# Gate and up of five feed-forward stages: three pairs of steps as seven block products, with weight sums on VectorE

## What is computed

```
def swiglu_2(x, w_gate, w_up, w_down):
    return (jax.nn.silu(x @ w_gate) * (x @ w_up)) @ w_down

def macaron_ffn(xs, g, shift, scale, gate, w_gate, w_up, w_down):
    return xs + 0.5 * gate * swiglu_2(modulate(xs, g, shift, scale), w_gate, w_up, w_down)
```

## Time and profile before

| what | value |
|---|---|
| median of 3 runs | 3579.99 us (3577.64 to 3580.52) |
| span of the profiled execution | 3574.0 us |
| TensorE busy (matmul) | 3487.5 us, 98% of the span, 18564 matmuls |
| VectorE busy | 2211.7 us, 62% |
| ScalarE busy | 1712.6 us, 48% |
| GpSimd busy | 113.8 us, 3% |
| mean granted TensorE clock | 0.997 of full |
| DMA | 654.63 MB, 183 GB/s over the span |

### The profile page before, as it was taken

One profiled execution on the slowest core, in us unless ns is written; L12 is line 12 of the kernel. 1 busy time (PEld: TensorE's weight loads), 2 busy tenths in 40 slices (PEclk: granted clock), 3 DMA queues, 4 the chain that ended last, 5 costly groups with the idle time before them and its releaser, 6 DMA issues. The chain is left out here.

```text
span 3574.0 us, 45127 instructions
## 1 busy us (share of the span) xinstructions
PE 3487.5 (98%) x18564; PEld 2960.8 (83%) x18564; DVE 2211.7 (62%) x2603; ACT 1712.6 (48%) x2073; POOL 113.8 (3%) x116
## 2 busy tenths in 40 slices
PE   9999999999999998999999999999999999999999
PEld 7889888888888887888889878888888678888887
DVE  5776656676667677576677555555556555545655
ACT  5454454544645446545454354545453454545543
POOL 0001100000000000000001100000000000000000
PEclk9999999999999999999999999999999999999999
DMA  7642156664476763676742145555554135454453
GB/s 271 239 154 79 60 202 234 216 231 176 156 271 252 258 226 123 224 282 227 280 178 93 60 177 189 182 184 183 183 175 154 60 142 189 172 189 164 156 209 130
DMA packets 90554, 654.63 MB, mean 183 GB/s; under 512 B 10096, under 2 KB 10224, under 8 KB 11632
## 3 DMA queue, kind: packets, MB, share of 16 engines
q1 hardware_dynamic: 79344, 574.15, 44.2%
q0 software_dynamic: 11008, 77.60, 6.0%
HBM read 650.66 MB, written 1.05 MB: 182 GB/s over the span
## 5 line engine op out<-in xcount | busy, mean ns | idle before, releaser
L2013 DVE TENSOR_TENSOR w_lo<-raw,w_hi 128x2048 fp32r<-128x2048 f32 x540 | 1234.2, 2290 | 614.5 <-ACT w_hi L1382 614.3
L1382 ACT ACTIVATE w_hi<-raw 128x2048 fp32r<-128x2048 f32 (+1 forms) x542 | 1032.7, 1909 | 499.2 <-PE acc L584 401.1
L582 PE MATMUL wrk<-w_hi,h_hi 128*128 128x512 f32 (+1 forms) x2400 | 939.6, 391 | 15.8 <-issue 5.4
L584 PE MATMUL wrk<-w_hi,h_lo 128*128 128x512 f32 (+1 forms) x2400 | 923.9, 385 | 0.0
L583 PE MATMUL wrk<-w_lo,h_hi 128*128 128x512 f32 (+1 forms) x2400 | 922.4, 384 | 0.0
L582 PEld LDWEIGHTS wrk<-w_hi,h_hi 128*128 128x128 f32 x2400 | 451.5, 188 | 105.2 <-issue 14.2
L584 PEld LDWEIGHTS wrk<-w_hi,h_lo 128*128 128x128 f32 x2400 | 451.3, 188 | 91.4
L583 PEld LDWEIGHTS wrk<-w_lo,h_hi 128*128 128x128 f32 x2400 | 452.1, 188 | 84.1 <-issue 0.2
L582 PE MATMUL acc<-w_hi,hid_hi 128*128 128x512 f32 (+1 forms) x1160 | 452.8, 390 | 4.6 <-DVE hid_lo L2115 4.5
L584 PE MATMUL acc<-w_hi,hid_lo 128*128 128x512 f32 (+1 forms) x1160 | 450.0, 388 | 0.0
L583 PE MATMUL acc<-w_lo,hid_hi 128*128 128x512 f32 (+1 forms) x1160 | 449.6, 388 | 0.0
(11 more groups left out here) (298 smaller groups left out, 4005.5 us busy)
## 6 DMA issues: line engine op xcount, KB each, us to landing
raw<-in_wts SPq DMA_DIRECT2D x541, 1024.0 KB, 4.8
arena<-in_mods POOLq DMA_DIRECT2D x72, 1024.0 KB, 5.1
const<-in_const SPq DMA_DIRECT2D x1, 2112.0 KB, 17.1
c<-in_bias POOLq DMA_DIRECT2D x8, 256.0 KB, 3.0
x<-in_x SPq DMA_DIRECT2D x2, 512.0 KB, 6.5
c<-in_c SPq DMA_DIRECT2D x1, 1024.0 KB, 4.8
out<-x SPq DMA_DIRECT2D x2, 512.0 KB, 2.6
row<-in_rows SPq DMA_DIRECT2D x1, 512.0 KB, 17.8
```

The lines of the kernel that those rows point to most:

```text
L582: nc.tensor.matmul(o, l_h, r_h, start=first, stop=False, skip_group_check=True)
L584: return nc.tensor.matmul(o, l_l, r_h, start=False, stop=last, skip_group_check=True)
L1382: return nc.scalar.activation(o, i, f, **kw)
L2013: tt(w_lo[:, ns % SLOTS, :], raw[:, ns % SLOTS, :], w_hi[:, ns % SLOTS, :].bitcast(F32), ALU.subtract).then_inc(lo_ready, 1)
```

## The change

Five stages get a new function `ffn_pairs` on each of the three engines. In it steps 2+3, 5+6 and 8+9 form **pairs**; the other five steps (0, 1, 4, 7, 10) stay as they were. Within a pair, gate (512 columns) and up (512 columns), by two halves of the inputs and two halves of the tokens, form a product of 2 x 2 blocks by 2 x 2 blocks, each weight block 512 inputs by 512 columns. Eight block products (96 matmuls) are replaced by seven (84), in the Winograd form of Strassen's scheme:

- Four sums of the token blocks, once a stage (`factors`, `factors_low`, with `x_hi` and `x_lo`).
- Four sums of weight blocks for each pair, on VectorE, 128 x 2048 each, in place in the arena: T1 = B11 + B12, T3 = B12 + B22, T2 = T1 + B22, T4 = B21 + T2 (`add_blocks`). B11 and so on are the loaded blocks; they land in four homes in the arena (`blocks`), not in `raw`.
- Seven ring pieces for a pair's gate and up where there were four: B11, B21, T2, T1, T3, T4, B22. Each is split to hi and lo as any piece.
- ScalarE copies bank A out three times (after B11, T2, T3); VectorE adds and subtracts these parts to form gate and up of both halves of tokens.

The adds for a pair stand in VectorE's queue in the step before it. TensorE does the `down` of steps that are "owed": one after a single step, two after a pair. `FINAL_AT` goes from 2 to 4, the look ahead of `b0_ctx` from 4 to 7, `GATE_AT` from 6 to 7. `rstd` becomes a part of `row`, whose load is moved from the start to ahead of `b0_ctx`; the last row lands in `c`. The scratch of the GpSimd DMA queue is set to 2048 bytes.

The diff, cut to what decides the order (names that are not shown stand in the kernel):

```diff
+FINAL_AT, CTX_AHEAD_AT, GATE_AT = 4, 7, 7
+
+PAIRS = {n: (2, 5, 8) for n in ("b0_ctx", "b0_ffn0", "b0_ffn1", "b1_ffn0", "b1_ffn1")}
...
+            items += [(b, s) for b in ("B11", "B21", "T2", "T1", "T3")] + [("d", owed[0])] + [("T4", s), ("B22", s)]
+            items += [("d", q) for q in owed[1:]]
...
+HOME = dict(B11=0, B12=1, B22=2, B21=3, T1=4, T3=1, T2=0, T4=3)
+HELD_BY = dict(B11="T4", B12="T3", B22="B22", B21="T4")
...
+                    if s == firsts[0]:
+                        sp.wait_ge(x_new, before(i, "x"))
+                        if before(i, "c"):
+                            sp.wait_ge(c_new, before(i, "c"))
+                    else:
+                        sp.wait_ge(lo_ready, ring_at[i, (HELD_BY[name], firsts[firsts.index(s) - 1])] + 1)
+                    sp.dma_start(blocks[HOME[name]], wts[k]).then_inc(block_landed[HOME[name]], 16)
```

TensorE, one pair, and the single step after or before it:

```diff
+                def pair(s, owed):
+
+                    g = number(s)
+                    a, b = bank(use[name, f"A{s}"]), None
+                    plain("B11", s, a, 0, 0, True)
+                    b = bank(use[name, f"B{s}"])
+                    plain("B21", s, b, 4, 0, True)
+                    for q in owed:
+                        turn_hid(q)
+                    pe.wait_ge(part_out, 3 * g + 1)
+                    summed("T2", s, a, False)
+                    o = bank(use[name, f"C{s}"])
+                    summed("T1", s, o, True)
+                    pe.wait_ge(part_out, 3 * g + 2)
+                    summed("T3", s, a, False)
+                    down_all(owed[0])
+                    pe.wait_ge(part_out, 3 * g + 3)
+                    plain("T4", s, a, 4, 1, False)
+                    pe.wait_ge(up_second, g + 1)
+                    summed("B22", s, o, False)
+                    for q in owed[1:]:
+                        down_all(q)
...
+                    gate_up(s, 0, 0, after)
+                    gate_up(s, 0, 1)
+                    for q in owed:
+                        turn_hid(q)
+                    gate_up(s, 1, 0)
+                    gate_up(s, 1, 1)
+                    for q in owed if s < STEPS - 1 else owed[:-1]:
+                        down_all(q)
+                    if "rows_first" not in prm and s == GATE_AT:
                         gate_rows(i, name, prm)
```

ScalarE, one pair, and the single step:

```diff
+                    split_to(n + 2)
+                    part("B11", s, part_a)
+                    split_to(n + 4)
+                    for q in owed:
+                        hid_high(q)
+                    part("T2", s, part_b)
+                    split_to(n + 5)
+                    act.wait_ge(gate_first, g + 1)
+                    fn(part_d, part_d, ACT.Silu).then_inc(e_ready, 1)
+                    split_to(n + 6)
+                    part("T3", s, part_c)
+                    split_to(n + 8)
+                    act.wait_ge(w_used, at("T4", s) + 1)
+                    fn(part_a, wrk[:, use[name, f"A{s}"] % BANKS, :], ACT.Silu).then_inc(e_ready, 1)
+                    split_to(n + 9)
...
+                    split_to(at("d", owed[-1]))
+                    silu_gate(s, 0)
+                    silu_gate(s, 1)
+                    if "rows_first" not in prm and s == GATE_AT:
+                        gate_rows(i, name)
+                    split_to(at("d", owed[-1]) + 1)
+                    if name == "b0_ctx" and s == FINAL_AT:
+                        nc.scalar.preload_act_table_set("natural_log_exp_and_others")
+                        statistics(op_at("final_norm"))
+                        nc.scalar.preload_act_table_set("silu_and_others")
+                    if name in AHEAD and s == (CTX_AHEAD_AT if name == "b0_ctx" else AHEAD_AT):
...
+                    split_to(at("d", owed[-1]) + 2)
```

VectorE, the single step (k = 1 is step 1), and one pair:

```diff
+                    split_to(at("d", owed[0]))
+                    for q in owed:
+                        hid_low(q)
+                    if k == 1:
+                        factors_low()
+                    split_to(at("d", owed[-1]))
+                    gated(s, 0)
+                    gated(s, 1)
+                    if ahead is not None:
+                        add_blocks("T1", ahead)
+                        add_blocks("T3", ahead)
+                    split_to(at("d", owed[-1]) + 1)
+                    if ahead is not None:
+                        add_blocks("T2", ahead)
+                    if name == "b0_ctx" and s == FINAL_AT:
+                        j = op_at("final_norm")
+                        final(j, *ops[j][1:])
+                    if s < STEPS - 1:
+                        split_to(at("d", owed[-1]) + 2)
+                    if ahead is not None:
+                        add_blocks("T4", ahead)
+                    if name in AHEAD and s == (CTX_AHEAD_AT if name == "b0_ctx" else AHEAD_AT):
+                        j = op_at(AHEAD[name])
+                        normalise(j, src=(c,) if ops[j][0] == "attn" else None)
...
+                    split_to(n + 4)
...
+                    tt(part_d, bank_of("B"), part_a, ALU.add).then_inc(gate_first, 1)
+                    for q in owed:
+                        hid_low(q)
+                    split_to(n + 6)
+                    dve.wait_ge(part_out, 3 * g + 3)
+                    tt(part_e, bank_of("C"), part_c, ALU.subtract).then_inc(up_second, 1)
+                    split_to(n + 8)
...
+                    tt(pair_hid[:, 1, :], part_e, part_a, ALU.mult).then_inc(taken, 2)
+                    dve.wait_ge(w_used, at("B22", s) + 1)
+                    tt(part_b, bank_of("C"), part_b, ALU.subtract).then_inc(taken, 1)
+                    dve.wait_ge(taken, use[name, f"C{s}"] + 1)
+                    tt(pair_hid[:, 0, :], part_b, part_d, ALU.mult).then_inc(pair_done, 1)
+                    split_to(n + 9)
```

More of the change, by code:

```diff
@@ L2010, in lo @@
             def lo(ns):
+                what, k = ring[ns]
+                v = raw[:, k % SLOTS, :] if what == "raw" else blocks[HOME[what]]
                 dve.wait_ge(hi_ready, ns + 1)
[L2013 removed]
+                tt(w_lo[:, ns % SLOTS, :], v, w_hi[:, ns % SLOTS, :].bitcast(F32),
                    ALU.subtract).then_inc(lo_ready, 1)
@@ L2948, in ffn_pieces, with block @@
     d = down.reshape(STEPS, 2, P, D).transpose(0, 2, 1, 3).reshape(STEPS, P, PW)
-    order = [g[0]]
-    for s in range(1, STEPS):
-        order += [g[s], d[s - 1:s]]
-    return order + [d[STEPS - 1:]]
+    def block(which, s):
+        w, half = (gate, up)[int(which[2]) - 1], int(which[1]) - 1
+        v = w.reshape(2, 4, P, F)[half, :, :, 256 * s:256 * s + NB]
+        return v.transpose(1, 0, 2).reshape(P, PW)
+    order = []
+    for item in load_items(name):
+        order.append(g[item[1], item[2]] if item[0] == "g" else d[item[1]] if item[0] == "d" else block(*item))
+    return [np.stack(order)]
 def out_pieces(w):
```

435 lines of the change are left out of this document (382 added, 53 removed).

## The result

| | before | after |
|---|---|---|
| median of the runs | 3580.23 us | 3601.76 us (3601.59 to 3602.16) |
| ratio, 95% interval | 1 | 1.0063 (1.0049 to 1.0077) |
| span of the profiled execution | 3574.0 us | 3600.0 us |
| mean granted clock in it | 0.997 | 0.992 |

The change makes the kernel slower by 21.5 us in the medians and by 26.0 us between the two profiled executions. The two differ because single executions of the kernel before lie between 3573.4 and 3582.8 us, and the profiled one, some 3575.8 us with the 1.8 us that lie around a span, is one of the shorter. One further execution of it took 4901 us at a mean granted clock of 0.663, a slow state that no figure here includes.

What follows compares the result with a forecast made beforehand. TensorE, busy 98% of the span, was taken as the bound: 55.8 us of new TensorE waits less 40.8 us of matmuls makes 15.0 us, span 3589 and time 3595 us, 0.4% slower; range 3570 to 3615 us.

Steps and rivals of the forecast that it cites:

- What is removed: Gate and up of 15 pairs: twelve matmuls fewer a pair at 0.227 us, so TensorE loses 40.8 us of work.
- First pairs: Each stage's first pair: T2 starts at E+16.9 (E: start of the first `down`), 5.7 us lost, 28.5 us in five stages.
- self-waits of 2.32 us: VectorE's adds and splits: start-to-start time where an operation waits for VectorE's own semaphore, against 2.21 us otherwise.
- Later pairs: Second and third pairs: T2 wanted at 16.7, ready at 16.9; 0.2 us lost in each of six, 1.2 us.
- `b0_ctx` and `b0_ffn0`, pairs 5: Side jobs on VectorE (final norm; attention norm's statistics and `normalise`) delay T2: 2.6 us lost in `b0_ctx`, 1.7 us in `b0_ffn0`.
- Pair 8: ScalarE's wait for gate rows stands ahead of B11's hi copy: 12.9 us lost in `b0_ctx`, 8.3 us in `b0_ffn0`.
- copied in time: Rival: ScalarE's wait for gate rows doesn't reach B11, 19 us less, 3576 us; chance 0.17, shared with smaller first-pair stalls.
- The waits together: New TensorE waits at the pairs: 28.5 + 1.2 + 2.6 + 1.7 + 8.3 + 12.9 us, 55.2 us without the opening.
- The opening: Start of a stage: four differences of x ahead of `gated` cost 0.2 us in three stages, 0.6 us in all.
- The clock: Rival: matmuls at 1.2 GHz after three stalls of about 5 us, 6 us in all, 3601 us; chance 0.22, shared with more stalls.
- 6 us lie around the span: Step from span to time: profiled span 3574.0 against median 3580.0 us, so a span of 3589 gives 3595 us.
- all hidden: Rival: VectorE's added work, some 58 us a stage, stays hidden behind TensorE, giving 3539 us; chance 0.11 for hidden or nearly.

Runs made afterwards that it cites:

- a_narrow_adds: Changed kernel with the four adds of weight blocks working on only 16 of 2048 columns, waits and order kept: 3561.17 us, ratio 0.9954 to the kernel before.
- e_two_pairs: Changed kernel with pairs at steps 5 and 8 only, steps 2 and 3 single: 3613.99 us, ratio 1.0105 to the kernel before.
- b_rows_late: Changed kernel with ScalarE's copies of the gate rows moved behind the hi copies of B11 and B21: 3581.14 us, ratio 1.0011 to the kernel before.
- c2_x_first: Changed kernel with x_hi and x_lo placed first in SBUF, ahead of the weight slots: 3595.88 us, ratio 1.0054 to the kernel before.
- i_new_order: h_three_edits with a third order on VectorE: T1, split B11, T2, split B21, T3, split T2, T4 later: 3575.76 us, ratio 0.9993.
- h_three_edits: Changed kernel with gate rows copied late, x_hi and x_lo first in SBUF, and b0_ctx's and b0_ffn0's look-ahead statistics at step 10: 3576.31 us, ratio 0.9993.

## Why the prediction was right, and where its sum was off

The forecast was 3595 us, slower by 15 us in the span; it is 3601.8 us, and 26.0 us in the span. The direction, the places and the mechanisms hold. Point by point:

- *What is removed*: 180 matmuls, 40.8 us; right. An addition takes 2.29 us, as taken from the earlier trace rows; VectorE comes to 69% of the span, forecast about 70%.
- *First pairs*: waits of 2.38, 1.63 and 1.17 us against 2.4, 1.5 and 1.3, though B21's wait stands in two stages only. T2 starts at E+17.17, where 16.9 was forecast: 5.94 us lost instead of 5.7, 1.2 us in five stages. Mis-sized was "self-waits of 2.32 us": that was read off an operation of 0.69 us, and behind these operations of 2.29 us the next one starts 2.39 to 2.42 us after the one before (2293.95 to 2296.34, 2298.55 to 2300.97). `a_narrow_adds` shows that the sums are the cause, `e_two_pairs` that it is the owed `down`.
- *Later pairs*: the step "T2 is wanted at 16.7 and ready at 16.9, lost 0.2 us" was mis-sized. Timeline of after, T2 of a later pair in `b1_ffn0`:

```profile
3198.82 0.60 PE L953 MATMUL wrk<-const,arena 128*128 128x128 f32 x4
3199.66 0.47 PE L698 MATMUL wrk<-w_hi,x_hi 128*128 128x512 f32 x1 [0.24 <-issue]
```

  From the transposes to T2 it is 0.84 us, where after nothing late it is 0.35: 0.49 us lost. The wait shown is 0.24, since the records of the transposes reach 0.25 us into the time. T2 starts at E+17.16 here, as in the first pairs: the same chain and the same mis-sized self-waits. In the six pairs it is 2.9 us instead of 1.2.
- *`b0_ctx` and `b0_ffn0`, pairs 5*: 2.9 and 1.8 us against 2.6 and 1.7.
- *Pair 8*: in `b0_ctx` B11 was forecast at E+17.6 and T2 at E+31.3; they start at E+17.7 and E+31.3 (E = 2387.68). In `b0_ffn0` T2 is at E+26.9 against 26.7. `b_rows_late` took 20.6 us away, where the sum had priced the rows at 8.3 + 11.0. The rival "copied in time" fell with the copy's wait of 11.38 us in the trace of after.
- *What the sum lacked*: the pitch of the 48 matmuls of a pair that read `x_hi` and `x_lo`, 0.233 instead of 0.227 us. I had priced all matmuls from the earlier trace rows, which read `h_hi` and `h_lo`; for the two new tiles the trace of before has no row, and no bound was put on them. 5.0 us, by `c2_x_first`.
- *The waits together*: by the start of each T2 the pairs lose 29.7 us (first), 2.9 (the six later ones), 4.7 (pairs 5) and 21.4 us (pairs 8), 58.7 in all against 55.2 forecast. The waits view shows 48 us in the five stages, 41 of them new: what TensorE needs to start up again and its slow products are no waits there.
- *The opening*: forecast 0.2 us in each of three stages. Up to the first `down` of step 1 it is 0.4 us in `b0_ffn1` and `b1_ffn0` and 0.1 us in `b1_ffn1`; the ends of these stages make up for some of it.
- *The clock*, a rival: it falls as the rival says and costs nothing where the rival says. Behind both waits of 4.90 us the records are longer (0.76 us; 0.63 in the earlier trace rows), and the granted clock is lower. Windows view of pair 8, `b0_ctx` and then `b0_ffn0`:

```profile
2406.00:2414.00 8.00, 4.69 (x14) 3.50 (x13) 4.89 (x3) 7.91 (x9) 0.00 (x0) 0.71 0.00 1
2414.00:2422.00 8.00, 8.00 (x28) 6.21 (x27) 8.00 (x6) 3.08 (x3) 0.00 (x0) 0.72 0.00 0
...
2606.00:2614.00 8.00, 5.36 (x14) 4.26 (x15) 7.56 (x4) 4.13 (x4) 0.00 (x0) 0.57 0.00 0
```

  But what is slow here stands ahead of a wait for VectorE. In `b0_ctx` B11 ends later, and the wait for B21 is 3.31 us where the sum had 4.8. In both stages T2 starts 0.1 us behind the end of its split (2418.97 behind 2418.88, 2617.82 behind 2617.73), as it does at full clock. In the first pairs the clock falls behind the 2.38 us ahead of B11 in three stages, and T2 starts at E+17.17 in all five. A slow product ahead of another wait is hidden by it. One behind the last wait is not, as `i_new_order` shows with 1.6 us. The Trainium skill, "TensorE: Matmul & The Clock Gate", section "Why this matters for your kernels", warns of lower throughput behind idle gaps; here the clock does fall behind them, in three stages of five behind the same 2.38 us (matmul record of 0.77 us at 2500.67 in `b0_ffn0`, 0.47 us at 2296.39 in `b0_ctx`). The rival's price of 6 us gave 3601 us, next to the measured 3601.8; that is chance.
- *The unchanged stages*: counted at nothing, they brought 2.4 us. 1.0 us lies ahead of `b0_ctx`, in code that is the same in both kernels, and shows in one window, before and then after, in which after falls back by 1.5 us:

```profile
2004.00:2012.00 8.00, 6.00 (x42) 5.81 (x41) 4.00 (x11) 4.28 (x4) 2.35 (x1) 0.79 0.01 2
```

```profile
2004.00:2012.00 8.00, 6.00 (x29) 5.81 (x29) 3.00 (x9) 4.28 (x4) 2.35 (x1) 0.60 0.01 2
```

  Another 1.1 us is the attention, with two falls of the clock instead of none, and 0.3 us the convolution.
- *From span to time*: "6 us lie around the span" was wrong. In each execution some 1.8 us lie around it (3601.84 against 3600.0). The other 4.2 us were the distance of a short execution from the median. That error made, by luck, the forecast of the time better than that of the span (6.8 us off, and 11).

Added up by stage: forecast +13.0 and measured +14.45 in `b0_ctx`, +7.5 and +9.12 in `b0_ffn0`, -5.6 and +0.05 in the other three, 0 and +2.4 elsewhere: 11.0 us. Of these the pitch makes 5.0, the unchanged stages 2.4, and the chains on VectorE 3.6 (1.2 at first pairs, 1.7 at the six later ones, 0.7 at pairs 5 and 8).

The rival "all hidden" would have meant 3539 us. The Trainium skill's rule in "Perfetto Trace Analysis", section "Identifying the Most-Contended Engine", names the engine to look at first. Read as the prediction read it, that less work on that engine is time won, it leads to the rival, and the runs speak against it: the second engine stood at 62% before and 69% after, and yet the change lost. `a_narrow_adds` gets to 3561 us by shortening nothing but VectorE's work.

In `b1_ffn0` the account nearly closes: 8.16 us saved; 5.94 us at the first pair, 2 x 0.49 at T2 of the later ones, and 3 x 0.36 for the pitch (the difference between after and `c2_x_first` there) are 8.0 us spent. The opening costs 0.4 us more, the end of the stage 0.2 us less; the stage is 191.33 us before and 191.34 after. The clock falls in it once, during B11, at no cost.

What stays open: what about a tile's place sets the pitch; why the clock falls behind a wait in one stage and not behind the same wait in another; what the third order would give if VectorE's T4 came in time. No kernel that does the whole computation beat the one before by more than can be told. The nearest are `h_three_edits` and `i_new_order`, at 0.9993.

## What to carry to other kernels

When work is moved from the busiest engine to one with room on average, write down the order of both queues around the point where they meet, with each operation's length, the hops over third engines too (here sum, ScalarE's copy, split): the opening of a group, where little other work is owed, sets the price. After a wait the matmuls may run at the lower clock, so a wait is best placed where another stands behind it. A copy that waits for the bounding engine belongs behind everything that this engine wants next. And for every new operand and every helper engine put a bound in the sum, even if no row of the old trace shows it; "the same instruction on another tile" was worth 5 us here, and a sum on GpSimd cost VectorE more than doing it itself.
